# Feed-forward with gate and up turned: weights stationary, high and low activations side by side as one moving operand

## What is computed

```python
D_FF = 2816
def rms_norm(x, g):
    y = xf * lax.rsqrt(jnp.mean(xf * xf, axis=-1, keepdims=True) + EPS)
    return y * g
def swiglu(x, w_gate, w_up, w_down):
    return (jax.nn.silu(x @ w_gate) * (x @ w_up)) @ w_down
# first_block, for i in range(DEPTH):
    x = x + 0.5 * swiglu(rms_norm(x, ffn1_norm[i]), ffn1_w_gate[i], ffn1_w_up[i], ffn1_w_down[i])
    ...
    x = x + 0.5 * swiglu(rms_norm(x, ffn2_norm[i]), ffn2_w_gate[i], ffn2_w_up[i], ffn2_w_down[i])
# second_block:
    h = rms_norm_2(x, norm_g[layer]) * (1.0 + scale) + shift
    x = x + gate * (m @ w_out[layer])
```

## Time and profile before

| | before |
|---|---|
| median of 3 runs | 1368.29 us (1368.06 to 1369.15) |
| the profiled execution: its time, its span | 1369.46 us, 1367.7 us |
| PE busy, weight loads | 1349.9 us (99%), 1143.5 us (84%) |
| DVE, ACT, POOL busy | 879.1 us (64%), 709.1 us (52%), 311.6 us (23%) |
| chain that ended last | PE 93%, DVE 3%, ACT 1%, issue 1%, DMA 1% |

### The profile page before, as it was taken

The page is one execution under the profiler, slowest core; times in us unless marked ns, Lnnn a source line. Parts: engine busy times, 40 slices in busy tenths (PEclk is TensorE's granted clock), DMA queues, the critical chain, the costliest instruction groups (busy, mean ns, idle before and its releaser), DMA issues.

```text
span 1367.7 us, 19554 instructions
## 1 busy us (share of the span) xinstructions
PE 1349.9 (99%) x7599; PEld 1143.5 (84%) x7599; DVE 879.1 (64%) x910; ACT 709.1 (52%) x838; POOL 311.6 (23%) x232
## 2 busy tenths in 40 slices
PE   8999999999999999999999999999999999999997
PEld 7888888878888888888899988888888898888885
DVE  5544468856445564555487999665877557776586
ACT  6444455655444454444466679654343455557443
POOL 3300001000000000000000036149995002525740
PEclk9999999999999999999999999999999999999999
DMA  9555545525555556555444564589765455545341
GB/s 296 190 191 191 194 146 193 185 93 192 192 193 190 185 165 197 190 186 184 154 155 159 198 229 161 179 323 323 264 231 191 139 175 161 189 157 176 115 158 42
DMA packets 158285, 254.09 MB, mean 186 GB/s; under 512 B 8784, under 2 KB 99232, under 8 KB 156560
## 3 DMA queue, kind: packets, MB, share of 16 engines
q1 hardware_dynamic: 155136, 232.94, 51.8%
q0 software_dynamic: 2576, 18.45, 3.7%
q10 hardware_dynamic: 512, 1.85, 0.4%
HBM read 252.12 MB, written 1.08 MB: 185 GB/s over the span
## 4 chain that ended last, share of the span: by engine, by line
PE 93%; DVE 3%; ACT 1%; issue 1%; DMA 1%; SPq 0%; POOL 0%; POOLq 0%; DVEq 0%; ACTq 0%
PE psum L607 11%; PE psum L609 11%; PE psum L608 11%; PE psum L644 5%; PE psum L642 5%; PE psum L643 5%; PE psum L1807 4%; PE psum L1808 3%; PE psum L1809 3%; PE psum L448 3%; PE psum L449 3%; PE psum L450 3%; PE psum L427 3%; PE psum L429 3%; PE psum L428 3%; DVE w_lo L389 2%
## 5 line engine op out<-in xcount | busy, mean ns | idle before, releaser
L389 DVE TENSOR_TENSOR w_lo<-raw,w_hi 128x2048 fp32r<-128x2048 f32 x220 | 546.1, 2487 | 325.4 <-ACT w_hi L381 325.1
L381 ACT ACTIVATE w_hi<-raw 128x2048 fp32r<-128x2048 f32 x220 | 421.4, 1916 | 341.6 <-PE psum L609 124.6
L607 PE MATMUL psum<-w_hi,hT_hi 128*128 128x512 f32 x704 | 278.8, 396 | 2.9 <-DVE w_lo L389 2.2
L609 PE MATMUL psum<-w_hi,hT_lo 128*128 128x512 f32 x704 | 274.6, 390 | 0.0
L608 PE MATMUL psum<-w_lo,hT_hi 128*128 128x512 f32 x704 | 274.2, 389 | 0.0
L607 PEld LDWEIGHTS psum<-w_hi,hT_hi 128*128 128x128 f32 x704 | 132.2, 188 | 31.3 <-DVE w_lo L389 3.7
L505 POOL TENSOR_TENSOR meansq<-sumsq 128x2 f32<-128x2 f32 x7 | 1.4, 194 | 683.1 <-ACT xn L473 683.1
L609 PEld LDWEIGHTS psum<-w_hi,hT_lo 128*128 128x128 f32 x704 | 132.1, 188 | 28.3
L608 PEld LDWEIGHTS psum<-w_lo,hT_hi 128*128 128x128 f32 x704 | 132.4, 188 | 26.3
L642 PE MATMUL psum<-w_hi,hidT_hi 128*128 128x512 f32 x320 | 124.9, 390 | 0.0
L644 PE MATMUL psum<-w_hi,hidT_lo 128*128 128x512 f32 x320 | 124.7, 390 | 0.0
(11 more groups left out here) (376 smaller groups left out, 2155.5 us busy)
## 6 DMA issues: line engine op xcount, KB each, us to landing
raw<-in_ffn_w_down SPq DMA_DIRECT2D x88, 512.0 KB, 4.2
raw<-in_ffn_w_gate SPq DMA_DIRECT2D x87, 512.0 KB, 4.0
raw<-in_ffn_w_up SPq DMA_DIRECT2D x87, 512.0 KB, 4.9
raw<-in_w_in SPq DMA_DIRECT2D x72, 512.0 KB, 4.6
raw<-in_ssm_w_in SPq DMA_DIRECT2D x48, 512.0 KB, 4.5
raw<-in_attn_w_qkv SPq DMA_DIRECT2D x24, 512.0 KB, 4.6
ada_in<-in_w_ada POOLq DMA_DIRECT2D x8, 1536.0 KB, 8.1
raw<-in_ssm_w_out SPq DMA_DIRECT2D x16, 512.0 KB, 4.6
```

What stands on the lines that cost most here:

```text
L381: act.activation(w_hi[:, slot, :], raw[:, slot, :], ACT.Copy).then_inc(sem("hi_ready"), 1)
L389: dve.tensor_tensor(w_lo[:, slot, :], raw[:, slot, :], w_hi[:, slot, :].bitcast(F32), ALU.subtract)\
L607: pe.matmul(to, a, hi[:, kk, :], start=k == 0, stop=False)
L609: m = pe.matmul(to, b, hi[:, kk, :], start=False, stop=k == KD - 1)
```

## The change

Gate and up are separate units now, each with all eight slices k (`columns`). The weights are the stationary operand and the activations the moving one, so the result comes out turned already (hidden columns on the partitions, tokens along the free side) and `turn` is gone. `hT_hi` and `hT_lo` are two halves of one tile `hT`; one matmul of 512 columns moves both past w_hi, and one of 256 columns moves hT_hi past w_lo into the first half of the same bank. The bank's two halves are added outside: ACT copies the second half out (`gate_part`, `up_part`), DVE adds the first (`gate_sum`, `up_sum`). Since the tokens lie along the free side, `rstd` can't be a scale per partition: POOL makes a diagonal (`rstd_diag`), two fp32 matmuls with ones turn it into a row (`row_of_rstd`), DVE multiplies the gate with it (`gate_scale`), and up's factor is applied at the very end (`half_rstd`). The order on PE is gate(c), down(c-1), up(c). In the last chunk PE does gate, up, down(NFC-2), and then the last down.

Other changes: in the norms the mean's factor goes into the squares and one of the POOL instructions runs before the last squares; the first unit and the norms ahead of the later feed-forwards make all eight hT slices earlier; `mod_pe` uses 64 columns in place of one; `split_hi` of one unit at the start of the second block moves behind the work on h; `turn_m(0)` moves into the last projection unit, ahead of its last slice, and DVE's `lo_of_m(0)` moves one step forward.

```diff
-        hT_hi = keep("hT_hi", [P, KD, SEQ], R32)
-        hT_lo = keep("hT_lo", [P, KD, SEQ], R32)
+        hT = keep("hT", [P, 2, KD, SEQ], R32)
+        hT_hi, hT_lo = hT[:, 0, :, :], hT[:, 1, :, :]
...
+                    act.activation(xn[:, t, cs], x[:, t, cs], ACT.Square, scale=D ** -0.5, accum_out=sumsq[:, h, t:t + 1])\
...
+            pool.wait_ge(sem("sumsq"), 4 * n + 2)
+            order(pool.tensor_scalar(meansq[:, :], sumsq[:, 0, :], 1.0, EPS, ALU.mult, ALU.add))
...
-            order(pool.tensor_scalar(meansq[:, :], meansq[:, :], 1.0 / D, EPS, ALU.mult, ALU.add))
+            order(pool.tensor_tensor(meansq[:, :], meansq[:, :], sumsq[:, 1, :], ALU.add))
...
+            pool.wait_ge(sem("const1_in"), 32)
+            pool.tensor_scalar(half_rstd[:, :], rstd[:, :], 0.5, 0.0, ALU.mult, ALU.add)
+            for t in range(TT):
+                pool.tensor_scalar(rstd_diag[:, t, :], ident, rstd[:, t:t + 1], 1.0, ALU.mult, ALU.mult)\
+                    .then_inc(sem("rstd_diag"), 1)
...
-                hT_lo_tiles(dve, n, gain, range(4, KD))
+                if not all_first:
+                    hT_lo_tiles(dve, n, gain, range(4, KD))
             for unit in late:
                 split_lo(dve, unit)
 
...
+                columns(u0 + 5, gate, c, c - 2, 3)
+                down_rows(u0 + 6, c - 1, c - 2, 3)
+                columns(u0 + 7, up, c, c - 2, 3)
...
-                        elif u + h == 0:
-                            use_unit(pe, 0)
-                        if first:
-                            pe.wait_ge(sem("hT"), KD * n + k + 1)
-                        for t in range(TT):
-                            to = psum[:, banks[t], :]
-                            a, b = hT_hi[:, k, t * P:(t + 1) * P], hT_lo[:, k, t * P:(t + 1) * P]
-                            pe.matmul(to, a, hi[:, kk, :], start=k == 0, stop=False)
-                            pe.matmul(to, a, lo[:, kk, :], start=False, stop=False)
-                            m = pe.matmul(to, b, hi[:, kk, :], start=False, stop=k == KD - 1)
-                    m.then_inc(sem("unit_used"), 1)
...
+            def columns(u, banks, step=0, per=0, ready=False):
...
+                    for i in range(2):
+                        both = psum[:, banks[i], :].rearrange("p (s n) -> p s n", s=2)
+                        a, b = (part[:, k, i * P:(i + 1) * P] for part in (hi, lo))
+                        if k:
+                            pe.matmul(both[:, 0, :], b, hT_hi[:, k, :], start=False, stop=False, skip_group_check=True)
+                        m = pe.matmul(both, a, hT[:, :, k, :], start=k == 0, stop=k == KD - 1, skip_group_check=True)
+                        if k == 0:
+                            pe.matmul(both[:, 0, :], b, hT_hi[:, k, :], start=False, stop=False, skip_group_check=True)
+                m.then_inc(sem("unit_used"), 1)
+
+            def gate(u, c, step=0, per=0):
+                pe.wait_ge(sem("ffn_read"), 2 * (done + c) - 1)
+                columns(u, GATE_BANKS, step, per)
+
...
+            def row_of_rstd():
+                pe.wait_ge(sem("rstd_diag"), TT * (FFNS.index(f) + 1))
+                for t in range(TT):
+                    m = pe.matmul(psum[:, RSTD_BANK, t * P:(t + 1) * P], row_ones[:, :], rstd_diag[:, t, :], start=True, stop=True)
+                m.then_inc(sem("rstd_turned"), 1)
...
-            def turn(c):
-                for t in range(TT):
-                    pe.wait_ge(sem("ffn_hid"), TT * (NFC * FFNS.index(f) + c) + t + 1)
-                    for k in range(2):
-                        m = pe.transpose(psum[:, 2, k * SEQ + t * P:k * SEQ + (t + 1) * P],
-                                         hid[:, t, k * P:(k + 1) * P], ident)
...
+            columns(u0, GATE_BANKS, ready=True)
+            columns(u0 + 1, UP_BANKS)
+            row_of_rstd()
+            gate(u0 + 2, 1)
+            down(u0 + 3, 0, first=True)
+            up(u0 + 4, 1)
             with pe.Fori(2, NFC - 1) as c:
-                gate_up(u0 + 5, c, c - 2, 3)
-                down(u0 + 7, c - 1, c - 2, 3)
-                turn(c)
-            gate_up(u0 + 3 * NFC - 4, NFC - 1)
-            down(u0 + 3 * NFC - 2, NFC - 2, ks=(0,))
-            turn(NFC - 1)
-            down(u0 + 3 * NFC - 2, NFC - 2, ks=(1,))
...
+            def gate_part(u, c, step=0, per=0):
                 act.wait_ge(sem("unit_used"), place(u, step, per)[0] + 1)
...
-                else:
...
-                    act.activation(silu_g[:, t, :], psum[:, banks[t], 0:FC], ACT.Silu, scale=rstd[:, t:t + 1])\
-                       .then_inc(sem("ffn_silu"), 1)
-
...
             with act.Fori(2, NFC - 1) as c:
+                gate_part(u0 + 5, c, c - 2, 3)
                 split_hi(act, u0 + 5 + SLOTS, c - 2, 3)
-                gate(u0 + 6, c, c - 2, 3)
+                silu(c)
                 split_hi(act, u0 + 6 + SLOTS, c - 2, 3)
+                up_part(u0 + 7, c, c - 2, 3)
                 split_hi(act, u0 + 7 + SLOTS, c - 2, 3)
-                turned(c)
+                hidden_hi(c)
+            gate_part(u0 + 3 * NFC - 4, NFC - 1)
...
-            def times_up(c, first=False, banks=GU_BANKS):
...
-                    dve.wait_ge(sem("ffn_silu"), TT * (NFC * FFNS.index(f) + c) + t + 1)
-                    dve.scalar_tensor_tensor(hid[:, t, :], psum[:, banks[t], FC:2 * FC], rstd[:, t:t + 1],
-                                             silu_g[:, t, :], ALU.mult, ALU.mult).then_inc(sem("ffn_hid"), 1)
-
...
+            def gate_sum(c):
+                dve.wait_ge(sem("ffn_part"), 2 * (done + c) + 1)
+                b = GATE_BANKS[0]
+                dve.tensor_tensor(silu_g[:, :, :], psum[:, b:b + 2, 0:SEQ], silu_g[:, :, :], ALU.add)\
+                   .then_inc(sem("ffn_read"), 1)
+
+            def gate_scale(c):
+                dve.wait_ge(sem("ffn_read"), 2 * (done + c) + 1)
+                row = rstd_row[:, :].unsqueeze(1).broadcast_to([P, 2, SEQ])
+                dve.tensor_tensor(silu_g[:, :, :], silu_g[:, :, :], row, ALU.mult).then_inc(sem("gate_scaled"), 1)
+
+            def up_sum(c):
+                dve.wait_ge(sem("ffn_part"), 2 * (done + c) + 2)
+                b = UP_BANKS[0]
+                dve.tensor_tensor(hid[:, :, :], psum[:, b:b + 2, 0:SEQ], hid[:, :, :], ALU.add)\
+                   .then_inc(sem("ffn_read"), 1)
+
+            def times_gate(c):
+                dve.wait_ge(sem("ffn_read"), 2 * (done + c) + 2)
+                dve.wait_ge(sem("ffn_silu"), done + c + 1)
+                dve.tensor_tensor(hid[:, :, :], hid[:, :, :], silu_g[:, :, :], ALU.mult).then_inc(sem("ffn_hid"), 1)
+
+            def hidden_lo(c, hi=hidT_hi, lo=hidT_lo):
+                dve.wait_ge(sem("ffn_hidT_hi"), done + c + 1)
+                dve.tensor_tensor(lo[:, :, :], hid[:, :, :], hi[:, :, :].bitcast(F32), ALU.subtract)\
+                   .then_inc(sem("ffn_hidT"), 1)
+
+            gate_sum(0)
             split_lo(dve, u0 + SLOTS)
-            times_up(0, first=True)
...
             with dve.Fori(2, NFC - 1) as c:
+                gate_sum(c)
+                gate_scale(c)
                 split_lo(dve, u0 + 5 + SLOTS, c - 2, 3)
-                times_up(c)
                 split_lo(dve, u0 + 6 + SLOTS, c - 2, 3)
+                up_sum(c)
+                times_gate(c)
                 split_lo(dve, u0 + 7 + SLOTS, c - 2, 3)
-                turned(c)
+                hidden_lo(c)
+            gate_sum(NFC - 1)
...
+                    dve.scalar_tensor_tensor(x[:, t, cs], psum[:, 4 + 2 * t + h, :], half_rstd[:, t:t + 1], x[:, t, cs],
...
+        MOD_WIDTH = 64
+
         def mod_pe(pe):
+
             for j in range(2 * KD):
-                m = pe.matmul(psum[:, 3, j:j + 1], ada[:, j * P:(j + 1) * P], ones[:, 0:1], start=True, stop=True)
+                m = pe.matmul(psum[:, 3, j:j + MOD_WIDTH], ada[:, j * P:(j + 1) * P], ones[:, 0:MOD_WIDTH],
+                              start=True, stop=True)
...
+                    if i == TICKS - 1 and kk == 3:
+                        turn_m(0)
                     for t in range(TT):
...
-                turn_m(n)
+                if n:
+                    turn_m(n)
...
-            norm_act(act, 6, None, False, FIRST_UNIT["in2"] - 1 + SLOTS)
+            norm_act(act, 6, None, False)
...
+            split_hi(act, FIRST_UNIT["in2"] - 1 + SLOTS)
...
-                order(pool.tensor_tensor(meansq[:, ts], sumsq[:, 0, ts], sumsq[:, 1, ts], ALU.add))
-                order(pool.tensor_scalar(meansq[:, ts], meansq[:, ts], 1.0 / D, EPS, ALU.mult, ALU.add))
+                order(pool.tensor_tensor(meansq[:, ts], meansq[:, ts], sumsq[:, 1, ts], ALU.add))
                 pool.tensor_tensor(rstd[:, ts], meansq[:, ts], neg_half[:, ts], ALU.pow).then_inc(sem("rstd"), 1)
...
                 if i == TICKS - 1:
+                    lo_of_m(dve, 0)
                     normed(dve, 1, out_b, None, (1,))
-                    lo_of_m(dve, 0)
                     mix(dve, c, 1)
```

262 lines of the change are left out of this document (142 added, 120 removed).

## The result

The changed kernel takes **1391.24 us** (median of 4 runs, 1391.11 to 1392.3) against 1368.72 for the kernel before in the same comparison: ratio 1.0159, 95% interval 1.0144 to 1.0173. It is slower, as forecast, but by 22.5 us and not by 7.6, and it lies above the range of 1362 to 1388.

What follows compares the result with a forecast made beforehand. PE's own instruction list was taken to bound the kernel. Feed-forwards -3.6, collision +15, POOL's table of angles in the first feed-forward +0.5 and the rest -4.3 gave +7.6: 1375.9 us from 1368.29, own range 1371 to 1382, wider 1362 to 1388.

Steps and rivals of the forecast that it cites:

- the 2.3 at the second block: Start of the second block: full clock with 64-column matmuls, and split_hi out of ACT's way, save 2.3 us.
- The fourth feed-forward: +15: Fourth feed-forward: DVE's waits for POOL now delay PE; 17 us taken, less 2 already there before.
- rival 3: Fourth feed-forward: PE's long waits make the clock fall two or three times; +8 us, 1384; chance 0.15.
- -3.6: Four feed-forwards without collision: -12.8 for matmuls, +1.4 row_of_rstd, +7 wait at down, +0.8 activation table.
- -4.3: Outside the feed-forwards' bodies: norms -0.3 and -0.7, start of second block -2.3, projection's wait for mT_lo -1.0.
- 32 x 0.2264 + 32 x 0.1200 = 11.09: Gate and up of a chunk on PE: 11.09 us after the change in place of 10.87.
- The other edits: 0.: Rounds of hT slices and loads: they lie beside PE work of the same length and cost 0.
- -0.3 and -0.7: Norm ahead of the state-space mixer and last norm: each loses one POOL instruction from its chain, saving these us.
- Rival 1: Fourth feed-forward: the collision is cheap, under 0.6 us per chunk; +15 becomes +2, 1362.9 us; chance 0.15.
- rival 5: At down: no wait, ACT or DVE being 0.2 us quicker; -7 us, 1369 with the collision, 1356 without; chance 0.07.
- Rival 2: Fourth feed-forward: each DVE wait ends with one POOL instruction; 1.3 us per chunk, +9 net, 1370; chance 0.12.
- Rival 4: Gate and up: a matmul's two 256-column pieces cost as two matmuls; +19 us, 1383; chance 0.03.

Runs made afterwards that it cites:

- e15: kernel before with 64 columns in place of one in the sixteen modulation matmuls, nothing else; 1370.24 us, ratio 0.9999.
- e10: kernel before with only the edits outside the feed-forward's body (norms, hT slices, mod_pe, split_hi, turn_m); 1366.60 us, ratio 0.9976.
- e12: changed kernel with one column in place of 64 in the sixteen modulation matmuls; 1393.12 us, ratio 1.0177.
- e3: changed kernel with hidden_hi and hidden_lo ahead of the third split on ACT and DVE, chunks 1 to 10; 1377.89 us, ratio 1.0051.
- e11: changed kernel with 448 bytes left free ahead of the work area, so its tiles shift by 2048 bytes, not 1600; 1389.10 us, ratio 1.0157.
- e6: kernel before without POOL's products and additions for modulation pieces 1 to 7, loads paced, last addition kept; 1367.44 us, ratio 0.9978.
- e5: changed kernel without POOL's products and additions for modulation pieces 1 to 7, loads paced, last addition kept; 1377.52 us, ratio 1.0055.
- e4: changed kernel with hT laid out so a slice's high and low columns are one contiguous run of 512; 1393.98 us, ratio 1.0185.
- e7: changed kernel with POOL waiting for each of its modulation instructions before issuing the next; 1393.24 us, ratio 1.0168.

## Why the prediction was right in sign and wrong in size

**Right.** The places: a wait for `hidT_lo` at each down, and the collision of DVE and POOL in the fourth feed-forward as the term that decides. The way from up to down (5.77 us) held to a hundredth, its cost nearly (0.19; 0.20 at down itself, 0.22 over the chunk). So did the price of two pieces (0), `row_of_rstd` (0.36 us from its start at 22.49 to gate's at 22.85) and the 2.3 at the second block (e15 and e10), though there the cause held only in the kernel before: in the changed kernel one column is as fast (e12).

**Wrong, by 14 us in two terms.**

1. *"The fourth feed-forward: +15" was mis-sized: it measured +18.1.* The step that failed is the account of what POOL does there. Its cycle of POOL, three `tensor_scalar` and three `tensor_tensor`, leaves out the last addition, 1x3072, which cost 3.9 net. And the clock at half after PE's three longest waits, 4.5, was rival 3 (0.15) and not in the sum; it is no rival to the collision but follows from it. What the term did count, the waits for the pieces, measured 9.7 in place of 15. So it is luck that 15 lies as near to 18.1 as it does. The prediction also had nearly all of the waiting fall on `split_lo`. Of 53 us 22.5 did, 17.7 fell on `gate_scale`, which costs PE little, and 13 on `times_gate` and `hidden_lo`, which costs it nearly all. By the page of the Trainium skill that the prediction named (SBUF — State Buffer, "Who interferes with whom") a wait ends with one instruction. The 6.72 us at 983.47 last through three, and with them 23 others, so the measurement speaks against that.

2. *Outside of any collision the four feed-forwards were summed to -3.6, and the rest to -4.3 (+0.5 for the angles): -7.4 in all; it measured +3.5.* Three steps failed, and together they make some 9 of the 10.9 us.
   - *"32 x 0.2264 + 32 x 0.1200 = 11.09" and "24 x 0.2264".* The distances were taken from uniform rows of matmuls and added. Mixed, a pair takes 0.3523 in up and 0.3469 in gate (sum: 0.3464), and down 0.2278 without a wait ahead of it (e3). That is 16 x 0.006 + 16 x 0.0005 + 24 x 0.0014 = 0.13 to 0.14 per chunk, and e3, without the wait, has 16.65 for 16.52: 0.13. With the wait's 0.22 it is the 16.87 measured. Over 44 chunks 0.13 is some 6 us, nearly half of a gain of 12.8; the wait's 0.22 for 0.19 adds 1.
   - *"The other edits: 0."* New tiles shifted the state-space mixer's operands: 1.2 us there, 0.5 behind the fourth feed-forward (e11). The prediction didn't look at addresses at all.
   - *"-0.3 and -0.7" for the norms.* The last norm gave 0.3. The start of the program (+0.6) differs as much between kernels of one kind. Some 1.5 us more, part of them between the third and the fourth feed-forward, stay open.

The two errors have the same sign, and the forecast's own range (1371 to 1382) had only the collision's bounds in it, none for the matmul distances, though the margin of 0.29 per chunk was called thin. A bound of 0.006 on each pair is 32 x 44 x 0.006 = 8 us, and with rival 3's 8 the range would have reached 1375.9 + 8 + 8 = 1392.

**The rivals.** Rival 1 (collision cheap) and rival 5 (no wait) fell by e5, e6 and e3. Rival 2 (one instruction's lock) fell as a mechanism, by the waits through three; its price, +9 net, is near the 9.7 that the pieces cost. Rival 3 came true beside the forecast: three falls of the clock, 4.5 us for its 8. Rival 4 fell by e4.

## What to carry to other kernels

When a change takes the slack away between two engines, price every disturbance on that way as new, even one that is fully covered now: one 6.8 us instruction cost nothing in the old feed-forward (e6) and 7.7 us in the new one (e5). Ask which instruction the disturbance will meet: 6.7 us on one that PE doesn't wait for cost it no more than 0.8, as much as 0.83 on the one that it does wait for. Where VectorE and GpSimd both work from SBUF, weigh the work moved to VectorE outright (27 us, in its gaps) against the same work beside it on GpSimd (126 us, and 13.5 of PE's). And a gain of 2% per step, summed from distances between matmuls, needs the distance of the very mixture and order, and tiles that keep their addresses.

## What the runs showed of the hardware

- A VectorE instruction with both inputs in SBUF can wait through a whole row of three GpSimd additions: 24 times in seven profiles, 5.8 to 7.5 us each. In these profiles that happened only in rows directly behind a load that GpSimd issued, for arrivals from 0.47 us before to 1.15 after the row's start. In rows without a load ahead 14 arrivals, 0.38 to 1.22 us after the start, waited for the first addition alone. The cause isn't shown.
- After TensorE had stood at a down for 2.20 us (e7) to 7.04 us (e7) the granted clock was at half during that down, and it took 1.3 to 2.9 us longer (the changed kernel, e4, e5, e7, e11, e12). After 2.18 us (e7) and less it was not.
- The same stationary operand shifted by 1600 bytes: 0.2333 us between 512-column matmuls in place of 0.2267; shifted by 2048, 0.2267.
- A pair of 512 and 256 columns in the loop: 0.353 to 0.354 us with the wide one first, 0.3469 or 0.3523 with the narrow one first.
- One-column matmuls were followed by the half clock in three profiles and by the full clock in a fourth.
